# Second projection: paced operand sums, other DMA queues for row stores and early loads, and a reordered column plan

## What is computed

```python
h = rmsnorm(h_res, norm_w) * (1 + scale) + shift
proj = h @ w_in + b_in          # 1024 -> 4*512 + 5*512 + 16
na_q, na_k, na_v, na_z, ml_q, ml_k, ml_v, ml_o, ml_z, i_f, f_f, i_b, f_b = split(proj)
na_out = neighbourhood_attention(na_q, na_k, na_v, rpb) * silu(na_z)
mq, mk = split(silu(centred_short_conv(concat(ml_q, ml_k), conv_w, conv_b)))   # 5 taps over tokens
h_fwd, h_bwd = mlstm_chunkwise(mq, mk, ml_v, i, f), and the same flipped
out = concat(na_out, norm((h_fwd + h_bwd) * sigmoid(ml_o)) * ml_norm_w * silu(ml_z)) @ w_out
```

## Time and profile before

| what | value |
|---|---|
| median of 3 runs | 1917.78 us (1914.2 to 1919.72) |
| the profiled execution | 1915.7 us |
| its span, first to last instruction | 1913.9 us |
| PE busy | 1849.9 us (97%) |
| DVE, ACT, POOL busy | 1086.0, 693.2, 577.1 us |
| mean granted TensorE clock | 0.986 |

### The profile page before, as it was taken

The page is one execution under the profiler, slowest core; times in us unless marked ns, Lnnn a source line. Parts: engine busy times, 40 slices in busy tenths (PEclk is TensorE's granted clock), DMA queues, the critical chain, the costliest instruction groups (busy, mean ns, idle before and its releaser), DMA issues. The chain is left out here.

```text
span 1913.9 us, 26831 instructions
## 1 busy us (share of the span) xinstructions
PE 1849.9 (97%) x9891; PEld 1522.9 (80%) x9891; DVE 1086.0 (57%) x2229; ACT 693.2 (36%) x1392; POOL 577.1 (30%) x942
## 2 busy tenths in 40 slices
PE   9999999999999999979989979999999999999998
PEld 8888878888888877857878867788886777788887
DVE  6556465675667335453242253465854777676675
ACT  7321111133445322121110121344735666655552
POOL 2112223224633102321111122112223777544442
PEclk9999999999999999989999989999998999999999
DMA  6223242366988527995246648487767776866763
GB/s 197 89 78 117 64 134 81 107 207 229 313 260 262 159 94 181 268 217 134 68 147 201 182 157 290 157 239 245 216 208 234 212 236 234 298 210 228 241 226 110
DMA packets 302414, 360.18 MB, mean 188 GB/s; under 512 B 42950, under 2 KB 211814, under 8 KB 302252
## 3 DMA queue, kind: packets, MB, share of 16 engines
q1 hardware_dynamic: 258188, 259.36, 44.6%
q0 software_dynamic: 37184, 90.72, 15.9%
q10 hardware_dynamic: 6912, 8.39, 1.3%
HBM read 251.34 MB, written 133.75 MB: 201 GB/s over the span
## 5 line engine op out<-in xcount | busy, mean ns | idle before, releaser
L145 PE MATMUL banks<-hT,wu 128*128 128x512 f32 (+1 forms) x528 | 204.6, 387 | 1.8 <-DVE wu L506 1.2
L147 PE MATMUL banks<-hT,wu 128*128 128x512 f32 (+1 forms) x528 | 202.3, 383 | 0.0
L146 PE MATMUL banks<-hT,wu 128*128 128x512 f32 (+1 forms) x528 | 202.2, 383 | 0.0
L145 PE MATMUL banks<-wub,iT 128*128 128x512 f32 x384 | 155.3, 404 | 17.4 <-DVE wub L1434 11.3
L146 PE MATMUL banks<-wub,iT 128*128 128x512 f32 x384 | 151.4, 394 | 0.0
L147 PE MATMUL banks<-wub,iT 128*128 128x512 f32 x384 | 151.1, 393 | 0.0
L2211 PE MATMUL banks<-fx,ft 128*128 128x512 f32 x336 | 131.0, 390 | 1.4 <-issue 0.8
L2213 PE MATMUL banks<-fx,ft 128*128 128x512 f32 x336 | 130.7, 389 | 0.0
L2212 PE MATMUL banks<-fx,ft 128*128 128x512 f32 x336 | 130.7, 389 | 0.0
L145 PEld LDWEIGHTS banks<-hT,wu 128*128 128x128 f32 x528 | 99.3, 188 | 26.1 <-ACT ub L470 4.3
L1609 DVE TENSOR_TENSOR st<-banks,br 128x512 f32<-128x512 f32 x48 | 33.1, 690 | 147.3 <-PE banks L147 140.1
(11 more groups left out here) (329 smaller groups left out, 4528.4 us busy)
## 6 DMA issues: line engine op xcount, KB each, us to landing
wa<-in_w_ada SPq DMA_DIRECT2D x48, 256.0 KB
iraw<-in_w_in SPq DMA_DIRECT2D x24, 512.0 KB, 5.8
fts<-wsum SPq DMA_DIRECT2D x36, 256.0 KB, 3.6
yT<-sg POOLq DMA_DIRECT2D x32, 256.0 KB, 3.1
oraw<-yT SPq DMA_DIRECT2D x32, 256.0 KB, 5.0
xr<-in_x SPq DMA_DIRECT2D x16, 512.0 KB, 4.1
h<-h POOLq DMA_DIRECT2D x16, 512.0 KB, 4.2
hT<-tr POOLq DMA_DIRECT2D x16, 512.0 KB, 5.0
```

The source lines that it names most:

```text
L145: e.matmul(ps, lh, rh, start=first, stop=False)
L146: e.matmul(ps, lh, rl, start=False, stop=False)
L147: return e.matmul(ps, ll, rh, start=False, stop=last)
```

## The change

1. **Plan.** The first pass holds nz 0 to 2, mk 0 and mk 1. Items 24 to 43 are mk 2, mk 3, mq 0, mq 1, mq 2; items 60 to 63 are mq 3; items 80 to 83 are nz 3. For the two k units of the first pass, whose items of one token block follow each other, there are four `cu` buffers for the first eight convolutions, and the edge columns come from two convolutions back.
2. **Weight jobs.** From item 20 on at most one unit is queued behind an item, so those of nv stand behind items 59, 60, 61 and 62, and those of mo behind 79 to 82.
3. **Sums.** Copies and adds are both on POOL's queue, spread over items 10 to 60: a weight sum's copy behind items 10, 12, ... 26, an activation sum's behind 28, 32, ... 56, each add four items after its copy. The copy no longer waits for PE.
4. **Row stores** of nv move from SP to ACT.
5. **Early loads** of `Fast` move from SP to ACT and are spread: behind items 2, 3, 4, 5, 7, 9, 11 and 13 of mo.
6. **States.** POOL's part of a step (`swv`) stands ahead of the item's store instead of behind it. The five-bank rotation starts one item earlier (43), PE's wait for the reserved banks stands behind item 43 (the last users are items 40 to 42), and the gate steps start two items earlier; the state steps start at item 63 as before.

```diff
-PLAN = [("nz", 0), ("nz", 1), ("nz", 2), ("nz", 3), ("mk", 0), ("mk", 1), ("mk", 2), ("mq", 0), ("mq", 1), ("mk", 3),
-        ("mv", 0), ("mv", 1), ("mv", 2), ("mv", 3), ("mq", 2), ("nv", 0), ("nv", 1), ("nv", 2), ("nv", 3), ("mq", 3),
+PLAN = [("nz", 0), ("nz", 1), ("nz", 2), ("mk", 0), ("mk", 1), ("mk", 2), ("mk", 3), ("mq", 0), ("mq", 1), ("mq", 2),
+        ("mv", 0), ("mv", 1), ("mv", 2), ("mv", 3), ("mq", 3), ("nv", 0), ("nv", 1), ("nv", 2), ("nv", 3), ("nz", 3),
...
-            while nu < len(PLAN) and self.freed[self.prior[nu]] <= n + 1:
+            while nu < len(PLAN) and self.freed[self.prior[nu]] <= n + 1 and len(jobs) < first + (1 if n >= 4 * self.FIRST else 9):
...
-        self.g0 = g0 = next(n for n, x in enumerate(work) if x[0] == "mv")
+        self.mv0 = next(n for n, x in enumerate(work) if x[0] == "mv")
+        self.g0 = g0 = self.mv0 - 1
...
+            elif name == "nv":
+                self.values_store(e, w, n)
...
             if name == "mo":
+                fast.early_load(e, w, tb)
                 fast.early_act(e, w, tb)
...
+            states.pool(e, w, n)
             if name in ("mq", "mk"):
...
             fast.add(e, w, n)
-            states.pool(e, w, n)
+            fast.copy(e, w, n)
...
+    def sum_at(self, n):
+
+        x, odd = divmod(n - 10, 2) if n < 28 else divmod(n - 28 + 36, 4)
+        return x if not odd and 0 <= x < self.SUMS else None
...
-    def early_sp(self, e, w, m):
+    def early_load(self, e, w, m):
         proj = self.proj
         if m == 2:
             w.wait_ge(*proj.lo.ge(len(proj.jobs)))
             self.unit_load(e, self.rx, 0, 0, self.rx_in)
+        if m == 4:
             for i in range(2):
                 w.wait_ge(*proj.ca_st[i].ge(16))
             self.unit_load(e, self.r0, 0, 1, self.rx_in)
-        for i in {3: (5, 2), 7: (1, 3), 11: (4, 6)}.get(m, ()):
-            w.wait_ge(*proj.full.ge(proj.mo0 + m + 1))
-            self.tokens_load(e, w, 0, i)
+        if m in (3, 5, 7, 9, 11, 13):
+            w.wait_ge(*proj.full.ge(proj.mo0 + m // 4 * 4 + 4 if m % 4 == 3 else proj.mo0 + m // 4 * 4))
+            self.tokens_load(e, w, 0, {3: 5, 5: 2, 7: 1, 9: 3, 11: 4, 13: 6}[m])
...
-        self.g0 = proj.g0 + 1
-        self.s0 = self.g0 + 18
+        self.g0 = proj.g0
+        self.s0 = proj.mv0 + 19
```

More of the change, by code:

```diff
@@ L1232, in __init__ @@
         self.st = [k.at(f"st{i}", 184 + 2 * i, [P, W]) for i in range(2)]
-        self.cu = [k.at(f"cu{i}", 196 + 2.03125 * i, [P, 4 + W + 2]) for i in range(2)]
+        self.cu = [k.at(f"cu{i}", (196, 198.03125, 171, 173.5)[i], [P, 4 + W + 2]) for i in range(4)]
         self.ca = [k.at(f"ca{i}", 200.0625 + 2.03125 * i, [P, W + 2]) for i in range(2)]
@@ L1507, in buffer_free, with piece, row @@
             w.wait_ge(*self.v_st[i % 2].ge(self.v_stored(i - 2)))
+    TWO = 8
+    def piece(self, i):
+        return i // 2 if i < self.TWO else i % 4
     def edges(self, i):
-        return sum(2 if x % 4 == 3 else 1 for x in range(i))
+        return sum(2 if self.piece(x) == 3 else 1 for x in range(i))
+    def row(self, i):
+        return self.cu[i % 4 if i < self.TWO else i % 2]
     def act(self, e, fast, states):
@@ L1527, in act @@
                 bcol = (4 if name == "mq" else 5) * 4 + j
-                cu, ca = self.cu[i % 2], self.ca[i % 2]
+                cu, ca = self.row(i), self.ca[i % 2]
                 w.wait_ge(*self.full.ge(n + 1))
@@ L1531, in act @@
                     w.wait_ge(*self.conv_step.ge(5 * (i - 1)))
-                    if (i - 2) % 4 != 3:
+                    if i >= self.TWO + 2 and self.piece(i - 2) != 3:
                         w.wait_ge(*self.conv_u.ge(self.edges(i - 1) + 1))
+                    if i < 4:
+                        for x in range(2):
+                            w.wait_ge(*out.t_st[x].ge(8))
                 else:
@@ L1575, in dve @@
                 ch = (4 if name == "mk" else 0) + j
-                cur, prev, a = self.cu[i % 2], self.cu[(i + 1) % 2], self.ca[i % 2]
+                cur, prev, a = self.row(i), self.row(i - (2 if i < self.TWO else 1)), self.ca[i % 2]
                 left, right = (2 if tb == 0 else 0), (W + 2 if tb == 3 else W)
@@ L1852, with add @@
     SUMS = 17
-    def copy(self, e, w, n):
-        n -= 21
-        if 0 <= n < self.SUMS:
-            w.wait_ge(*self.proj.full.ge(n + 21))
-            if n >= 3:
-                w.wait_ge(*self.copy_in[n % 3].ge(n // 3))
-            dst, src, _ = self.sums(n)
-            e.dma_start(dst, src).then_inc(*self.copy_in[n % 3].inc())
-    def add(self, e, w, n):
-        n -= 26
-        if 0 <= n < self.SUMS:
-            w.wait_ge(*self.copy_in[n % 3].ge(n // 3 + 1))
-            dst, _, src = self.sums(n)
-            e.dma_start(dst, src, accum_op=ALU.add).then_inc(*self.added.inc())
+    def sum_at(self, n):
+        x, odd = divmod(n - 10, 2) if n < 28 else divmod(n - 28 + 36, 4)
+        return x if not odd and 0 <= x < self.SUMS else None
+    def add(self, e, w, n):
+        x = self.sum_at(n - 4)
+        if x is not None:
+            w.wait_ge(*self.copy_in[x % 2].ge(x // 2 + 1))
+            dst, _, src = self.sums(x)
+            e.dma_start(dst, src, accum_op=ALU.add).then_inc(*self.added.inc())
+    def copy(self, e, w, n):
+        x = self.sum_at(n)
+        if x is not None:
+            if x >= 2:
+                w.wait_ge(*self.copy_in[x % 2].ge(x // 2))
+            if x >= 9:
+                for i in range(2):
+                    w.wait_ge(*self.proj.out.t_st[i].ge(8))
+            dst, src, _ = self.sums(x)
+            e.dma_start(dst, src).then_inc(*self.copy_in[x % 2].inc())
     def columns(self, b, row, u):
```

28 lines of the change are left out of this document (13 added, 15 removed).

## The result

The changed kernel takes 1892.38 us at the median of 4 runs (1890.09 to 1894.57) against 1916.54 for the kernel before on the same chip: ratio 0.9873, interval 0.9853 to 0.9893, 24.2 us faster. The forecast was 1870, the range 1861 to 1888: right in direction, outside in size. The profiled execution is the 1894.57 us one, its span 1892.8 us, its mean granted clock 0.989.

A forecast was written before the change was run, and what follows sets the result against it. PE was taken to bound the kernel, with 53.5 us at most to win from its waits and low clock. 1915.7 - 53.5 + 0.5 + 3.9 + 0.5 + 0.4 + 0.8 + 1.3 = 1869.6, so 1870 us, range 1861 to 1888.

The forecast's parts named there:

- the sentence on the burst: Convolutions, items 24 to 43: a `ca` store 5.4 us after an add-and-copy burst of about 9 waits 2 us extra on DVE.
- My upper bound, 5.6 us: Convolutions: the most a `ca` store behind a burst would wait extra on DVE, the longest such wait in the earlier trace.
- bursts still hold the convolutions: Rival, 0.16: one queue for stores, adds and copies and a harder bank wait; stall 7.5 instead of 0.5, 1879 us.
- The sign of being wrong: In DVE's trace: the forecast is wrong if DVE still waits for `ca` stores by tens of us.
- `cu`, reserved banks: PE's wait behind item 43 for the convolutions' last bank: lag 5.5 us before item 42, stall 0.3, say 0.5 us.
- nv's fourth split, `wub`: PE's new wait at nv's first row: split complete at 26.1 us, PE ready at 22.3, stall 3.9 us.
- `skC`: A term of 0.4 us in the sum, for PE's wait named `skC`.
- `state`: mo's state waits of PE, 6.7 us before: spread early loads leave 0 to 1 us, taken as 0.5.
- gate step: The `mpB` wait of 4.1 us: steps two items earlier stand in mv's rows, one DVE pass per item; gone.
- loads' queue: Rival, 0.11: the early loads' queue doesn't matter, state stores land in 8 to 12 us, PE keeps its 6.7; 1877 us.
- ACT as the bound: Rival, 0.05: in nv's rows `skT`'s store stands behind four to six row stores; at 13 us of landing, 1930 us.
- The rival of the sums that are moved and not paced: Rival, 0.08: POOL held at issue, or copies crowd the first pass's `h` loads; half of 53.5 us stays, 1890 to 1900.

The follow-up runs named there:

- e3: The changed kernel with each activation sum's add six items behind its copy instead of four, so the 1 MB transfers stand two items apart; 1872.6 us.
- h1: The changed kernel with the eight activation sums' adds cut to 16 of 512 rows, copies and all else in place; 1871.8 us.
- e1: The changed kernel with the convolutions' `ca` stores issued by ACT right behind its Silu instead of by POOL; 1888.3 us.
- e2: The changed kernel with the activation sums moved out of the convolutions: copies behind items 44, 46 to 58, adds four items later; 1874.0 us.
- f1: The changed kernel with activation adds six items behind their copies, and nv's row stores back on SP; 1875.4 us.
- f3: The changed kernel with activation adds six items behind their copies, the old plan of units and no four-buffer convolutions in the first pass; 1876.0 us.
- f4: The changed kernel with activation adds six items behind their copies, and POOL's `swv` behind the item's store again; 1875.8 us.
- f6: The changed kernel with the convolutions' stores on ACT's queue, each issued behind the next item's evacuation; 1884.2 us.

## Why the prediction was wrong in size

**The step that failed** is the sentence on the burst: an add and a copy as "a burst of about 9" us, and from it 2 us of extra wait per store. The average behind it held: I predicted a share of 0.29 + 0.46 = 0.75, and the changed kernel stays below it, at 0.47 and 0.43 in the two stretches shown with e3, while e3, which runs without the stalls, shows 0.75 and 0.80. (The 0.29 was read from 700 to 720 us, which are still items of the first pass and the gates.) But I turned 10 us of work for all engines into a length of 9 as if they ran full from the first moment. They don't: 0.57 in the first 4 us, 0.99 and 1.07 only in the next eight, 14 us in all. The store behind it, issued 4.4 us into the burst, lands at its end. The waits are 4.45, 6.19 and 6.78 us in items 31, 35 and 39. The prediction named 35 and 39 as the places, and had 2 us for each, and nothing for 31; so 17.4 us stand where 4 were counted. Of these 13.4 us more, 10.8 came out as stall (11.3 against 0.5), and the rest was slack in the chain. My upper bound, 5.6 us from the earlier trace rows, was too low as well. The rival "bursts still hold the convolutions" was the true case, but it stood at 1879 with 7.5 us of stall, and the range, which ended at 1888, had room for it and not for its being too small. The sign of being wrong that I had given, waits for `ca` stores by tens of us, came: 22.4 us in the four waits up to item 43.

**The second step that failed** is not a term that was too small but terms that I didn't write down: who else loads or stores beside a burst. In the changed kernel's DVE timeline, in POOL's and SP's, and in the landing of tile `skC` from 940 to 1000 us:

```profile
877.85 0.69 DVE L1625 TENSOR_TENSOR st<-banks,br 128x512 f32<-128x512 f32 x1 [9.20 <-DMA mv<-st]
```

```profile
954.71 1.12 POOL L1882 DMA_DIRECT2D hsum<-hT  x1
```

```profile
956.71 0.80 SPq L2801 DMA_DIRECT2D skC<-mk  x1
```

```profile
DMA to landing us min/median/max: 2.6/3.0/13.5
```

DVE's row pass in mv waited 9.2 us for a store behind the pairs, and the gate step queued behind it cost PE 2.7 us, where I had written "gone". The keys of the state step were issued 2 us behind the add of item 60, landed in 13.5 us, and cost 5.2, where I had 0.4. Both vanish in e3 and h1. For the keys it isn't that a pair was split, since this add stands alone in both: in e3 it moved from item 60 to 62 and goes out at 950.3, 11.5 us behind the keys' load instead of 2 us ahead of it. One 1 MB transfer is enough where a load with no slack follows it.

Point by point, by the terms of the sum:

| term | predicted | changed kernel | with the pairs apart (e3) |
|---|---|---|---|
| `cu`, reserved banks | 0.5 | 11.3 | 0.3 |
| nv's fourth split, `wub` | 3.9 | 0.5, hidden behind `skC` | 4.2 |
| `skC` | 0.4 | 5.2 | 0 |
| `state` | 0.5 | 4.8 | 3.3 |
| gate step | 0 | 2.7 | 0 |
| first wait of the next stage | 0.8 | 0.8 | 0.8 |
| sum | 6.1 | 25.3 | 8.6 |

The profiled 1894.6 less the predicted 1869.6 is 25.0 us. 19.2 of it are waits, by this table. 2.4 are low clock: before, items without their waits and low clock took 635.0 - 44.2 - 8.5 = 582.3 us; here 610.5 - 24.5 = 586.0, so 3.7 where 1.3 was in the sum. 4.2 lie behind the items, 683.8 us against 679.6 before, and 0.8 is taken off since the items begin earlier (598.5 against 599.3). Of the 4.2 the wait for `fpart` took 1.6 (2.2 against 0.6). The rest I can't place. In e1, e2, f1, f3 and f4, whose code behind the items is the same, the stretch takes 679.6 to 680.0 us, but in e3, the same there too, 684.4. So it varies between executions of the same code and need not be the change's.

**What was right.** PE as the only engine that bounds; the `swv`, `mpB` and mv `wub` waits gone; no wait in the first pass; nv's split at 3.9 against 4.2 measured as soon as nothing hid it, from counting two queues against PE's 5.45 us. nv's stores on ACT cost PE nothing that shows, and tile `skT`'s transfers landed in 5.5 us at most in nv's rows; that the move wins nothing may be wrong, by some 3 us (f1, with intervals that overlap). With mo's loads spread, PE's state waits there fell from 6.7 to 1.3 us (the other 3.5 of the 4.8 us are two waits in items 82 and 83, 1.6 and 1.9). The reason I gave for it was wrong: I wanted `CD` landings below 7 us from the change of queue. Tile CD in the changed kernel, 1076 to 1215 us, answers to the earlier trace rows:

```profile
  DVE state L2847: 29.3, 10
...
DMA to landing us min/median/max: 2.1/3.9/10.0
```

The landings are nearly as long as before: the two longest are 10.0 and 7.5 us, where they were 11.7 and 8.4. A step's slack takes the 7.5 whole and leaves 1.3 us of the other, where PE waited 3.8 and 2.9. Of the rivals, the first happened; the "loads' queue" rival was right about the queue and not about the time; ACT as the bound didn't show. The rival of the sums that are moved and not paced has the measured time inside its 1890 to 1900, but by luck: PE waits nowhere in the first pass, and POOL isn't held at issue; where the sums still crowd is behind the pairs, which is the first rival again.

## What to carry to other kernels

Price a large transfer by what the small one behind it will see, not by its share of a stretch: list, for each 1 MB transfer, which store or load is issued in the next 15 us and how much slack its consumer has. Don't let two of them stand together if one alone fits the slack; moving the add two items off its neighbour was worth 16 to 20 us and changed no byte. And where a chain has 0.5 us per item in hand, a wait of 6 us takes some thirteen items to recover, and anything added to its links, an issue and the wait ahead of it as in e1, takes that recovery away.

## What the runs showed of the hardware

- Two 1 MB transfers in DRAM, a copy and an accumulate, issued 0.7 us apart, kept the 16 engines in work, with the small stores beside them, for some 14 us, at a share of 0.57 for the first 4 us and about 1.0 for the next 8. The activation sums' transfers landed after 10.5 to 14.0 us. With the adds apart (e3) they took 6.4 to 11.5.
- A 256 KB store landed in 3.7 us at the median and 2.5 at best, in 8.9 to 10.7 right behind an activation pair in the same queue, and in 7.8 to 9.0 in another engine's queue beside one (f6).
- A load in SP's queue, issued 2 us behind a single 1 MB add on POOL's, landed in 13.5 us, where 3.0 was the median of such loads.
- A DMA issue on ACT is 0.33 us, but behind ACT's own result it lengthened a chain by 0.55 us an item, since ACT waited 0.40 to 0.46 us more (e1); issued one instruction later, it cost nothing that could be seen (f6).
